# Two transformer-style blocks on one core: a new order for the opening, for three places in the middle and for the last two units

## The chip, the cores and the metric

The kernel runs on one core of a Trainium2 chip. The metric is device time in microseconds (us): the median of 3 runs of the kernel before is 921.19 us (920.6 to 923.35). All times in the rows are counted from the start of the span of one profiled execution.

Five engines work side by side, each in the order of its own program, and wait for each other by semaphores: PE (TensorE, the matmuls; PEld is its weight load), DVE (VectorE), ACT (ScalarE), POOL (GpSimd), and SP, which here only issues transfers. PE writes into eight banks of PSUM.

## The reference, cut to what matters

Everything is float32. The input is x of 256 positions by 1024 columns. The first block is

```
h = rms_norm(x, pre_mix);  proj = h @ w_in          # 3472 columns and a remainder of 16: gdn_a, gdn_b
o_att = attention(att_q, att_k, att_v, rel_bias)    # 8 heads, causal, one block of 256
qkv = silu(depthwise_conv4(gdn_qkv))                # 1536 columns
beta = sigmoid(gdn_b);  g = -exp(A_log) * softplus(gdn_a + dt_bias)      # "the gates", 8 heads
o_gdn = chunked gated delta rule over q, k, v, beta, cumsum(g)           # triangular solve, state
o_gdn = rms_norm(o_gdn per head) * norm_w * silu(z)                      # "the gated norm"
x = x + rms_norm([o_att, o_gdn] @ w_out, post_mix)
h = rms_norm(x, pre_mlp);  x = x + rms_norm(square(relu(h @ w_up)) @ w_down, post_mlp)
```

The second block is a gated convolution and a retention layer, mixed by w_o_2, and then

```
h2 = rmsnorm(x, g_ffn)
x = x + (silu(h2 @ w_ff_gate) * (h2 @ w_ff_up)) @ w_ff_down              # 11 tiles of 256 columns
return rmsnorm(x, g_final)
```

## The kernel before, in words

**Units.** The weights are cut into 144 units of 128 x 2048 values (the first, of kind Z, has 1024: the 128 columns that end with the gates' 16). SP loads unit after unit into three raw buffers. To keep the precision of float32, each unit is split: ACT casts it to a rounded leading part (`t_wh`, "hi", line 1100, or in two halves at line 1114), DVE subtracts (`t_wl`, "lo", line 1569, in halves at 1583). The activations are split in the same way into `t_hx` (hh and hl). Each product is three matmuls: leading by leading, leading by remainder both ways. ACT and DVE split units two ahead of the one that PE is at (`next_unit` in each engine's program); `t_wh` and `t_wl` have four buffers, so a split waits for PE only where it is four units ahead.

**Order.** There is no scheduler. Each engine's program is written out by hand, in one order, and a wait is set where an engine needs another's result. What an engine does late in its own order therefore holds up all that is written behind it.

**Banks.** PE asks for a bank with `take`. Without a number it gets the next of the banks 4 to 7 in rotation; with a number it gets that one. `opened` makes PE wait until the bank's last reader is done, and `drain` says who that reader is. Wide units first move the rotation to an even bank and take two.

**Opening (lines 580 to 636).** PE starts with 14 matmuls of constants (line 582), transposes the two scaled halves of x (`turn_x`, line 407, one half of the positions after the other), and makes a small matmul for the attention bias (line 590). Then come the unit Z, called "ab" here (line 430, 24 matmuls), and the six convolution units (48 matmuls each). ACT and DVE make hh and hl from the transposed x, eight products each (lines 1143 and 1595); each matmul step k waits for the k-th of DVE's. ab waits for its bank 4 too, whose last reader is DVE's second product. After convolution unit 0 PE transposes the gates (`t_dU`), and after unit 1 it sums them (lines 624 and 625). On DVE the gates' arithmetic stands behind the three taps of convolution unit 0 (1595), and on ACT behind that unit's copy and first tap (lines 1218, 1226), exps (1230 to 1234) and a logarithm (1236) with its table load.

**Middle.** The products kT with kq (line 701, eight banks' worth in four pairs, "KQ") are read by DVE, two operations per bank. The delta rule's inverse is made in levels with many 64 x 64 matmuls (726) between attention steps (660, 663, 686). `mend` (804) needs DVE's copy `t_cout` of line 1842 (`to_second_half`), which for c = 1 stands behind the gated norm of c = 0, and this norm contains a wait for a root on POOL (2172). `between` is the passage from one layer to the next, used twice ("mlp", "mix2"): ACT casts one unit in halves and one whole and then copies two banks (line 1178, to `t_up` or `t_vv`).

**End.** `a_pair` (line 515) makes the last two units of the feed-forward's down projection: 24 matmuls of tile t = 0 and then 24 of t = 1, in each of them 12 with the first unit and 12 with the second. The second unit needs `t_fl` of the last tile from DVE.

## Time and profile before

| | us |
|---|---|
| median of 3 runs | 921.19 (920.6 to 923.35) |
| profiled execution, its time | 920.38 |
| profiled execution, its span | 918.6 |
| PE busy | 898.2 (98%), 5456 matmuls |
| PEld busy | 764.6 (83%) |
| DVE busy | 603.1 (66%) |
| ACT busy | 461.0 (50%) |
| POOL busy | 91.0 (10%) |
| mean granted clock of TensorE | 0.996 |

The time contains 1.78 us outside the span (920.38 less 918.6). PE is idle for 20.4 us in all (918.6 less 898.2). In the rows below, a time in brackets is the idle time of the engine just before the instruction, with what released it; "x8" is a count of instructions merged into one row. A float32 matmul of constants or of another tile that is not rounded shows as two records.

### The profile page before, as it was taken

Reading aid. Unit: us, or ns where it says so; the run is one execution under the profiler, and the core shown is the slowest. Engines: PE = TensorE matmul, PEld = TensorE weight load, DVE = VectorE, ACT = ScalarE, POOL = GpSimd, SP = SyncE. Lnnn points to the kernel's source line nnn. Section 1 sums busy time; section 2 is a strip of 40 time slices with the busy share of each in tenths; the row PEclk is TensorE's granted clock in tenths of the full one; section 3 lists DMA queues with packets and bytes.
Section 4 is the critical chain, followed back from the end, with each engine's and each line's share of the span. In section 5 each row is a group of like instructions: output and inputs, shape, how many; then the busy total and the mean of one; then the engine's idle time right before and its main releaser. Section 6 shows DMA issues by size and latency. Waiting matters only on the chain.

```text
span 918.6 us, 12761 instructions
## 1 busy us (share of the span) xinstructions
PE 898.2 (98%) x5456; PEld 764.6 (83%) x5456; DVE 603.1 (66%) x704; ACT 461.0 (50%) x557; POOL 91.0 (10%) x92
## 2 busy tenths in 40 slices
PE   7999999999999999999999999999999999999996
PEld 7998888778888887888888878778788888888885
DVE  6689984676556667687767665556656656564655
ACT  6766365464445445654643354453455555444543
POOL 1124100100000000100034410110100000000000
PEclk9999999999999999999999999999999999999999
DMA  8635512335444455445474524544455346555531
GB/s 314 247 138 184 172 50 93 131 125 218 185 183 183 183 186 227 171 185 184 147 266 156 198 107 183 181 165 161 163 202 180 138 171 234 180 183 218 183 138 46
DMA packets 24217, 159.81 MB, mean 174 GB/s; under 512 B 3240, under 2 KB 3768, under 8 KB 5856
## 3 DMA queue, kind: packets, MB, share of 16 engines
q1 hardware_dynamic: 21600, 152.58, 45.6%
q0 software_dynamic: 2272, 6.24, 1.9%
q8 instruction: 43, 0.70, 0.3%
q10 hardware_dynamic: 288, 0.17, 0.1%
q14 instruction: 14, 0.11, 0.0%
HBM read 157.91 MB, written 2.63 MB: 175 GB/s over the span
## 4 chain that ended last, share of the span: by engine, by line
PE 76%; DVE 13%; ACT 6%; issue 2%; DMA 1%; POOL 1%; POOLq 0%; DVEq 0%; ACTq 0%
PE banks L490 32%; PE banks L458 20%; PE banks L461 10%; DVE t_wl L1569 5%; ACT t_wh L1100 2%; PE banks L515 2%; PE banks L430 2%; PE banks L726 2%; PE banks L980 1%; PE banks L407 1%; DVE t_cout L1595 1%; PE banks L570 1%; PE banks L930 1%; DVE t_hx L1595 1%; PE banks L1062 1%
## 5 line engine op out<-in xcount | busy, mean ns | idle before, releaser
L1569 DVE TENSOR_TENSOR t_wl<-t_raw,t_wh 128x2048 fp32r<-128x2048 f32 (+1 forms) x140 | 319.2, 2301 | 125.8 <-ACT t_wh L1100 124.6
L458 PE MATMUL banks<-t_hx,t_wh 128*128 128x512 f32 x992 | 312.2, 396 | 1.0 <-ACT t_vv L1178 0.5
L1100 ACT CAST t_wh<-t_raw 128x2048 fp32r<-128x2048 f32 (+1 forms) x140 | 262.6, 1900 | 12.0 <-DMA t_raw<-in_W 7.6
L461 PEld LDWEIGHTS banks<-t_hx,t_wl 128*128 128x128 f32 x992 | 186.3, 188 | 43.8
L461 PE MATMUL banks<-t_hx,t_wl 128*128 128x256 f32 x992 | 194.9, 278 | 0.0
L458 PEld LDWEIGHTS banks<-t_hx,t_wh 128*128 128x128 f32 x992 | 153.2, 189 | 4.0 <-DVE t_wl L1583 1.8
L490 PE MATMUL banks<-t_wh,t_hx 128*128 128x512 f32 x320 | 102.3, 396 | 0.0
L490 PEld LDWEIGHTS banks<-t_wh,t_hx 128*128 128x128 f32 x320 | 59.5, 188 | 12.7 <-issue 0.6
L430 PE MATMUL banks<-t_hx,t_wh 128*128 128x256 f32 x336 | 62.8, 289 | 1.5 <-DVE t_hx L1595 1.5
L490 PE MATMUL banks<-t_wl,t_hx 128*128 128x512 f32 x160 | 61.1, 390 | 0.0
L430 PEld LDWEIGHTS banks<-t_hx,t_wh 128*128 128x128 f32 x336 | 53.6, 196 | 2.6 <-DVE t_hx L1595 2.2
L2172 POOL TENSOR_TENSOR t_st<-t_st,t_half 128x1 f32<-128x1 f32 (+1 forms) x18 | 10.6, 589 | 435.0 <-DVE t_st L1595 433.2
L1419 ACT COPY t_hold<-banks 128x512 f32<-128x512 f32 x28 | 16.4, 584 | 68.6 <-PE banks L461 57.5
L430 PE MATMUL banks<-t_hx,t_wl 128*128 128x256 f32 x168 | 48.2, 287 | 0.0
L1378 ACT COPY t_tail<-banks 128x512 f32<-128x512 f32 x14 | 8.2, 586 | 55.6 <-PE banks L461 55.6
L490 PEld LDWEIGHTS banks<-t_wl,t_hx 128*128 128x128 f32 x160 | 30.1, 188 | 6.3 <-issue 0.2
L490 PE MATMUL banks<-t_wh,t_mh 128*128 128x512 f32 x112 | 34.6, 390 | 0.0
L490 PE MATMUL banks<-t_wl,t_mh 128*128 128x512 f32 x112 | 34.5, 389 | 0.0
L490 PE MATMUL banks<-t_wh,t_ml 128*128 128x512 f32 x112 | 34.5, 389 | 0.0
L430 PEld LDWEIGHTS banks<-t_hx,t_wl 128*128 128x128 f32 x168 | 32.9, 196 | 0.0
L1587 DVE TENSOR_TENSOR t_rl<-banks,t_tail 128x512 f32<-128x512 f32 x14 | 9.7, 690 | 28.4 <-ACT t_tail L1378 28.4
L2266 POOL TENSOR_SCALAR t_gt<-t_gt,t_small 128x256 f32<-128x256 f32 x16 | 14.6, 924 | 117.2 <-ACT t_gt L1477 105.3
(310 smaller groups left out, 1258.5 us busy)
## 6 DMA issues: line engine op xcount, KB each, us to landing
t_raw<-in_W SPq DMA_DIRECT2D x143, 1024.0 KB, 4.9
skew<-scr POOLq DMA_DIRECT2D x1, 1536.0 KB, 13.2
t_x<-in_x SPq DMA_DIRECT2D x2, 512.0 KB, 5.0
t_tab<-in_tab POOLq DMA_DIRECT2D x1, 640.0 KB, 6.1
out<-t_xt SPq DMA_DIRECT2D x2, 320.0 KB, 2.3
t_raw<-in_W SPq DMA_DIRECT2D x1, 512.0 KB, 6.8
t_T<-skew POOLq DMA_DIRECT2D x4, 128.0 KB, 2.4
t_xt<-skew POOLq DMA_DIRECT2D x4, 128.0 KB, 2.4
```

The source lines that it names most:

```text
L430: m = e.matmul(bank[b][:, c * S:c * S + S], W[w][:, h, k * 128 * nt + c * 128:k * 128 * nt + c * 128 + 128], H[a][:, k, :], start=first, s ...
L458: e.matmul(bank[b + c], M.wh[:, h, wk], M.hx[:, k, :, :].rearrange("p a s -> p (a s)"), start=k == 0, stop=False)
L461: m = e.matmul(bank[b + c][:, 0:S], M.wl[:, h, wk], M.hh[:, k, :], start=False, stop=k == 7)
L490: m = e.matmul(bank[outs[t][c]][:], act[a][:, ks[kk], t * 128:t * 128 + 128], W[w][:, h, kk * 512 * ncb + c * 512:kk * 512 * ncb + c * 512 ...
L515: m = e.matmul(bank[outs[t][c]][:], act[a][:, k, t * 128:t * 128 + 128], W[w][:, (i0 + u) % HR, kk * 1024 + c * 512:kk * 1024 + c * 512 + ...
L726: m = e.matmul(bank[b][p, i * 64:i * 64 + 64], left(p), right(p), start=True, stop=True)
L1100: e.copy(M.wh[:, h, 0:n], M.raw[:, r, 0:n]).then_inc(q.sem, q.tick(("hi", i)))
L1419: e.copy(halves(M.rest[:, s, :]), both(M.banks, at[tile], 1)).then_inc(q.sem, q.tick((tile, "rest")))
L1569: e.tensor_tensor(M.wl[:, h, 0:n], M.raw[:, r, 0:n], M.wh[:, h, 0:n].bitcast(F32), ALU.subtract).then_inc(q.sem, q.tick(("lo", i)))
L1595: return e.scalar_tensor_tensor(out=o, in0=a, scalar=s, in1=b, op0=op0, op1=op1).then_inc(q.sem, q.tick(*names))
L2172: return e.tensor_tensor(o, a, b, op).then_inc(q.sem, q.tick(*names))
L2266: e.tensor_scalar(M.gt[:, a, :], M.gt[:, a, :], gw[:, 4 * h + a:4 * h + a + 1], None, ALU.mult).then_inc(q.sem, q.tick(("gt", h, a)))
```

## The change

Eight edits, all of order and place; the products that reach the output are the same, and five matmuls of constants are added.

1. The 14 constant matmuls write bank 3 instead of 7. Four more stand between the transposes of the two halves of x, and one behind the bias matmul.
2. Unit Z (ab) takes bank 1 instead of the next in rotation. It is split in two halves of 512, by ACT and DVE. It and convolution unit 0 start on the leading halves (`hi`) and take the leading products of k = 0 to 3 first, then those with `t_wl`, then k = 4 to 7.
3. The gates are transposed in the middle of convolution unit 0, and their arithmetic on DVE and ACT stands ahead of that unit's taps and copy.
4. The bias tables lie in `t_PT` and `t_va` instead of `t_cout`, so ACT's taps wait neither for the bias row nor for its transfer; POOL clears the convolution's margin (`pad`) first.
5. KQ pairs 4 to 7 take the banks 0 to 3.
6. One cast of ACT moves from between two copies at level 1 of the inverse to between the two copies of `t_va`; in `between`, one cast moves to between the two copies of line 1178.
7. `to_second_half(1)` moves into the gated norm of c = 0, ahead of the wait for POOL's root.
8. In the last `a_pair`, six matmuls of t = 1 with the first unit stand ahead of the matmuls of t = 0 with the second (`ahead=6`).

Since ab and four KQ banks no longer come from the rotation, every bank taken from it up to the passage "mlp" is one place lower in the new kernel; from the wide units on both kernels have the same banks.

```diff
-            def b_unit(tile, arrived, by, name, kind="B", k_outer=False, mid=None, halved=False):
+            def b_unit(tile, arrived, by, name, kind="B", to=None, mid=None, halved=False):
...
-                q.wait_ge(DV, ("lo", i, 0) if halved else ("lo", i))
+                q.wait_ge(*((AC, ("hi", i, 0)) if halved else (DV, ("lo", i))))
...
+                if halved:
+                    order = steps(range(4), (0, 1)) + steps(range(4), (2,)) + steps(range(4, 8), range(3))
...
+                    if halved and n_ == 8 * nt:
+                        q.wait_ge(DV, ("lo", i, 0))
+                    elif halved and n_ == 12 * nt:
                         q.wait_ge(DV, ("lo", i))
...
+                order = [(t, n_) for t in range(2) for n_ in range(24)]
+                order = order[:12] + order[24:24 + ahead] + order[12:24] + order[24 + ahead:]
...
+            def constants(n):
+
+                q.wait_ge(PO, "half")
+                for i in range(n):
+                    e.matmul(bank[3][:, 0:128], M.half[:], M.half[:], start=True, stop=True)
...
+                    if t == 0:
+                        constants(4)
...
-            b_unit("ab", x_in, AC, "ab", "Z")
+            constants(1)
+            b_unit("ab", x_in, AC, "ab", "Z", to=1, halved=True)
...
-                b_unit(("conv", u), x_in, AC, ("cin", u), k_outer=u == 0, halved=u == 0,
-                       mid=queries_and_keys if u == 5 else None)
+                b_unit(("conv", u), x_in, AC, ("cin", u), halved=u == 0,
+                       mid=gates if u == 0 else queries_and_keys if u == 5 else None)
...
-                bs = [take(("KQ", g + w)) for w in range(2)]
+                bs = [take(("KQ", g + w), None if g < 4 else g + w - 4) for w in range(2)]
...
-                hi(unit[0] + 3)
-                unit[0] += 2
                 for t in range(2):
                     q.wait_ge(PE, ("first", g, t))
                     e.copy(dst[:, t, :], bank[at["first", g, t]][:]).then_inc(q.sem, q.tick(taken(t)))
+                    if t == 0:
+                        hi(unit[0] + 3)
+                        unit[0] += 2
...
                 e.copy(M.va[:, c, :], bank[at["va", c]][:]).then_inc(q.sem, q.tick(("va", c)))
+                if c == 0:
+                    next_unit()
...
                 if c:
                     lo_half(0)
+                else:
+                    to_second_half(1)
```

**PE's opening.** The names in the rows: `t_xt` is the scaled x, `t_hx` its transposed parts, `t_half` the constants; the row with 8x384 is the bias matmul, and the first row with `t_wh` opens ab. Before:

```order
L407 MATMUL banks<-t_ident,t_xt 128x128 [waits act_done]
L407 MATMUL banks<-t_ident,t_xt 128x128 x3
L407 MATMUL banks<-t_ident,t_xt 128x128 [waits dve_done]
L407 MATMUL banks<-t_ident,t_xt 128x128 x3
L407 MATMUL banks<-t_ident,t_xt 128x128 [waits act_done]
L407 MATMUL banks<-t_ident,t_xt 128x128 x3
L590 MATMUL banks<-t_cout 8x384 [waits in_rbT,in_onehot]
L430 MATMUL banks<-t_hx,t_wh 128x256 [waits dve_done]
L430 MATMUL banks<-t_hx,t_wh 128x256
L430 MATMUL banks<-t_hx,t_wl 128x256
```

In the new kernel the same place reads:

```order
L405 MATMUL banks<-t_ident,t_xt 128x128 x3
L543 MATMUL banks<-t_half 128x128 x4
L405 MATMUL banks<-t_ident,t_xt 128x128 [waits dve_done]
L405 MATMUL banks<-t_ident,t_xt 128x128 x3
L405 MATMUL banks<-t_ident,t_xt 128x128 [waits act_done]
L405 MATMUL banks<-t_ident,t_xt 128x128 x3
L601 MATMUL banks<-t_PT,t_va 8x384 [waits in_rbT,in_onehot]
L543 MATMUL banks<-t_half 128x128
L434 MATMUL banks<-t_hx,t_wh 128x256 [waits dve_done,act_done]
L434 MATMUL banks<-t_hx,t_wh 128x256
L434 MATMUL banks<-t_hx,t_wh 128x256 [waits dve_done]
L434 MATMUL banks<-t_hx,t_wh 128x256
```

Four and one constant matmuls have come in, and ab opens with pairs of leading matmuls, each pair with a wait of its own, where a matmul with `t_wl` stood third before.

**DVE around convolution unit 0.** `t_cout<-banks,t_cout` (new: `t_va<-banks,t_PT`) is the bias row, the rows of `t_wl` 128x2048 are the remainders of the units 2, 3 and 4, `t_gs` holds the gates, and `t_cout<-t_cin` are the taps. Before:

```order
L1587 TENSOR_TENSOR t_cout<-banks,t_cout 8x384 [waits in_neg,pe_done]
L1569 TENSOR_TENSOR t_wl<-t_raw,t_wh 128x2048 [waits act_done,raw_in2]
L1569 TENSOR_TENSOR t_wl<-t_raw,t_wh 128x2048 [waits act_done,raw_in0]
L1595 SCALAR_TENSOR_TENSOR t_cout<-t_cin,t_small,t_cout 128x256 [waits act_done] x2
L1595 SCALAR_TENSOR_TENSOR t_cout<-t_cin,t_small,t_cout 128x256 [waits dve_done] x4
L1587 TENSOR_TENSOR t_gs<-banks,t_small 128x16 [waits pe_done]
L1709 COPY t_gs<-banks 128x16
L1595 SCALAR_TENSOR_TENSOR t_gs<-t_gs 128x16 [waits dve_done]
L1591 TENSOR_SCALAR t_gs<-t_gs 128x16 [waits act_done]
L1715 RECIPROCAL t_gs<-t_gs 128x16 [waits dve_done]
L1595 SCALAR_TENSOR_TENSOR t_gs<-t_gs 128x16 [waits act_done]
L1595 SCALAR_TENSOR_TENSOR t_gs<-t_gs 128x16 [waits dve_done]
```

The same engine and place in the new kernel:

```order
L1600 TENSOR_TENSOR t_va<-banks,t_PT 8x384 [waits in_neg,pe_done]
L1582 TENSOR_TENSOR t_wl<-t_raw,t_wh 128x2048 [waits act_done,raw_in2]
L1600 TENSOR_TENSOR t_gs<-banks,t_small 128x16 [waits pe_done]
L1706 COPY t_gs<-banks 128x16
L1608 SCALAR_TENSOR_TENSOR t_gs<-t_gs 128x16 [waits dve_done]
L1582 TENSOR_TENSOR t_wl<-t_raw,t_wh 128x2048 [waits act_done,raw_in0]
L1604 TENSOR_SCALAR t_gs<-t_gs 128x16 [waits act_done]
L1715 RECIPROCAL t_gs<-t_gs 128x16 [waits dve_done]
L1608 SCALAR_TENSOR_TENSOR t_gs<-t_gs 128x16 [waits act_done]
L1608 SCALAR_TENSOR_TENSOR t_gs<-t_gs 128x16 [waits dve_done]
L1608 SCALAR_TENSOR_TENSOR t_cout<-t_cin,t_small,t_cout 128x256 [waits act_done] x2
L1608 SCALAR_TENSOR_TENSOR t_cout<-t_cin,t_small,t_cout 128x256 [waits dve_done] x4
```

The gates stand around the remainder of unit 3 and ahead of the six taps.

**DVE at the gated norm.** `t_gs<-t_kb` is the sum of squares, `t_cin<-t_cin,t_gs` the first product after POOL's root, and `t_cout<-banks 64x512` the copy that `mend(1)` needs. Before:

```order
L1866 TENSOR_REDUCE t_gs<-t_kb 128x8 [waits act_done]
L1591 TENSOR_SCALAR t_gs<-t_gs 128x8 [waits dve_done]
L1587 TENSOR_TENSOR t_cin<-t_cin,t_gs 128x512 [waits pool_done]
L1587 TENSOR_TENSOR t_cin<-t_cin 128x512 [waits dve_done]
L1842 COPY t_cout<-banks 64x512 [waits pe_done]
L1569 TENSOR_TENSOR t_wl<-t_raw,t_wh 128x2048 [waits act_done,raw_in1]
```

and in the new kernel:

```order
L1880 TENSOR_REDUCE t_gs<-t_kb 128x8 [waits act_done]
L1604 TENSOR_SCALAR t_gs<-t_gs 128x8 [waits dve_done]
L1856 COPY t_cout<-banks 64x512 [waits pe_done]
L1600 TENSOR_TENSOR t_cin<-t_cin,t_gs 128x512 [waits pool_done]
L1600 TENSOR_TENSOR t_cin<-t_cin 128x512 [waits dve_done]
L1582 TENSOR_TENSOR t_wl<-t_raw,t_wh 128x2048 [waits act_done,raw_in1]
```

The copy has moved up by two places, to the front of the wait for POOL.

## Rows read from the trace of the kernel before

**Rows 1.** The page, part 1: busy us, share of the span, instructions.
```profile
PE 898.2 (98%) x5456; PEld 764.6 (83%) x5456; DVE 603.1 (66%) x704; ACT 461.0 (50%) x557; POOL 91.0 (10%) x92
```

**Rows 2.** Waits of PE: engine, tile, line, releaser: us in total, times, longest.
```profile
PE banks L430 <- DVE t_hx L1595: 1.5, 1, 1.5
PE banks L804 <- DVE t_cout L1842: 1.4, 1, 1.4
...
PE banks L701 <- DVE t_dU L1587: 0.9, 2, 0.7
PE banks L515 <- DVE t_fl L1587: 0.9, 1, 0.9
...
PE banks L624 <- DVE t_gs L1595: 0.8, 1, 0.8
...
PE banks L458 <- ACT t_vv L1178: 0.5, 1, 0.5
...
PE banks L660 <- ACT t_xt L1311: 0.4, 1, 0.4
```

**Rows 3.** Matmuls of line 430 in three stretches: us, busy (count), PEclk, DMA.
```profile
12.84:23.07 10.23, 10.20 (x72) 10.18 (x72) 0.83 0.86 324
14.24:17.62 3.38, 3.38 (x18) 3.38 (x17) 0.51 0.75 305
23.20:29.20 6.00, 6.00 (x49) 5.79 (x48) 1.00 0.85 320
```

**Rows 4.** Timeline of the opening: start us, us, instruction [idle before <-releaser].
```profile
9.58 1.03 ACT L1100 CAST t_wh<-t_raw 128x1024 fp32r<-128x1024 f32 x1
...
10.71 1.23 DVE L1569 TENSOR_TENSOR t_wl<-t_raw,t_wh 128x1024 fp32r<-128x1024 f32 x1 [1.27 <-ACT t_wh L1100]
11.86 3.22 DVE L1595 SCALAR_TENSOR_TENSOR t_hx<-banks,t_small,t_hx 128x256 fp32r<-128x256 f32 x8
...
12.87 0.47 PE L430 MATMUL banks<-t_hx,t_wh 128*128 128x256 f32 x2 [1.55 <-DVE t_hx L1595]
...
17.22 0.37 ACT L1192 COPY t_dU<-banks 128x256 f32<-128x256 f32 x1
...
17.73 4.47 DVE L1569 TENSOR_TENSOR t_wl<-t_raw,t_wh 128x2048 fp32r<-128x2048 f32 x2
```

**Rows 5.** Timeline around the gates.
```profile
24.70 2.47 DVE L1595 SCALAR_TENSOR_TENSOR t_cout<-t_cin,t_small,t_cout 128x256 f32<-128x256 f32 x6 [2.50 <-ACT t_cout L1226]
...
27.94 1.28 ACT L1236 ACT_TABLE_LOAD   x1
...
30.01 0.36 PE L624 MATMUL banks<-t_gs,t_tab 128*128 128x16 f32 x2 [0.81 <-DVE t_gs L1595]
```

**Rows 6.** Two stretches: us, busy of PE, PEld, DVE, ACT, POOL, PEclk, DMA.
```profile
20.00:40.00 20.00, 19.19 (x160) 19.01 (x160) 12.21 (x24) 11.70 (x20) 3.45 (x6) 1.00 0.78 289
40.00:60.00 20.00, 20.00 (x168) 19.82 (x167) 18.99 (x39) 16.08 (x24) 0.00 (x0) 1.00 0.45 160
```

**Rows 7.** Timeline of PE where convolution unit 5's output is needed.
```profile
65.28 0.88 PE L407 MATMUL banks<-t_ident,t_cout 128*128 128x128 f32 x6 [0.56 <-ACT t_cout L1198]
```

**Rows 8.** Timeline where the inverse begins.
```profile
116.17 1.22 DVE L1587 TENSOR_TENSOR t_xt<-t_kb,t_tab 128x1024 f32<-128x1024 f32 x1
...
118.27 2.08 PE L726 MATMUL banks<-t_tab,t_xt 64*64 64x64 f32 x64
```

**Rows 9.** Timeline of ACT at level 1 of the inverse.
```profile
130.18 1.90 ACT L1100 CAST t_wh<-t_raw 128x2048 fp32r<-128x2048 f32 x1
```

**Rows 10.** Timeline of the gated norm of c = 0.
```profile
159.78 1.67 POOL L2172 TENSOR_TENSOR t_gs<-t_gs,t_half 128x8 f32<-128x8 f32 x1 [8.44 <-DVE t_gs L1591]
...
162.94 0.69 DVE L1842 COPY t_cout<-banks 64x512 f32<-64x512 f32 x1
```

**Rows 11.** Timeline of ACT at the end of the passage "mlp".
```profile
196.72 1.07 ACT L1178 COPY t_up<-banks 128x512 f32<-128x512 f32 x2
```

**Rows 12.** Timeline of DVE in the last stretch.
```profile
911.21 0.69 DVE L1587 TENSOR_TENSOR t_x<-t_x,banks 128x512 f32<-128x512 f32 x1 [1.19 <-PE banks L515]
```

188 lines of the change are left out of this document (90 added, 98 removed).

## The prediction, made before the changed kernel had run

> **What bounds the kernel now.** I read the page's first part for the busiest engine, then the waits of PE, then the timeline around each wait, and the windows for the clock. PE is busy for 898.2 of 918.6 us [rows 1]; the other engines matter only where PE waits for them. The reader is to see in the waits of PE that its 20.4 idle us are many small ones, of which seven kinds stand where this change has an edit [rows 2]. The windows show a loss that no wait shows: the granted clock is 0.51 from 14.24 to 17.62 us, the level of 1.2 GHz, and 1.00 afterwards, 2.4 GHz [rows 3]. So the time is a chain of PE's work, its short waits and one slow stretch, and I count what each edit takes out of this chain, and then whether another engine can follow.
>
> **Term 1, the opening (edits 1, 2 and 4): 2.0 us.** ab starts at 12.87 [rows 4]. DVE's eight products start at 11.86, when the remainder of unit Z is done, and last 3.22, 0.40 each [rows 4]. ab waits for two of them, since its bank 4 is read by the second. In the new kernel ACT casts 512 columns first. A cast of 1024 takes 1.03 and the DVE remainder 1.23 [rows 4]; half of each, with some 0.1 of fixed cost, is 0.6 and 0.65. The cast starts at 9.58, so the remainders run from 10.2 to 11.5 instead of 10.71 to 11.9, and the products start 0.35 earlier. Bank 1 is free, so ab waits for one product: 0.4 less. ab can then begin at 12.1, but each step waits for its product, and the last one is done at 11.5 + 3.22 = 14.7; three matmuls of 0.12 (6.00 us for 49, [rows 3]) and the way through the array end ab at 15.2. Convolution unit 0 follows with 48 x 0.12 = 5.76, and the gates' two transposes of some 0.25 together now stand inside it: unit 1 begins at 21.2 instead of 23.2 (72 matmuls in 10.23 us [rows 3], the transposes and their wait included behind them). Of these 2.0 us, 1.5 are the clock: 72 matmuls at 0.12 would take 8.7, not 10.2. The other 0.5 is the earlier start. Cover: unit 0's leading casts and first remainders are made by then (ACT has cast units 1 and 2 by 17.22, [rows 4]). The gates' transposes need ab's copy, which ACT makes at 17.22, behind these casts [rows 4]; PE comes to them at 15.2 + 24 x 0.12 = 18.1, so 0.9 us of cover is left, or 0.7 if the split cast costs ACT 0.2. Unit 1 needs the remainder of unit 2, which DVE starts at 17.73 and has after half of 4.47, at 20.0 [rows 4], before 21.2. The four constant matmuls stand in a pause of 1.2 us between the transposes and cost nothing unless the clock is low there; bounds 0 to 0.4. Edit 4 takes waits from ACT only, which is idle again before PE needs it; POOL's clearing comes before loads that PE does not wait for now, so I count nothing. Bounds of the term: 0.5 to 2.3.
>
> That the clock stays up is the open point. It fell at 14.24 after a stretch in which PE had only transposes, one bias matmul and pauses (the one before ab is 1.55, [rows 4]). Now five more matmuls lie in it, and ab starts 0.8 sooner. The Trainium skill, page "TensorE: Matmul & The Clock Gate", Part 4: PE-mode transpose, says that transposes do not count as work for the clock; the trace agrees in so far as the clock fell behind them. The same page, Part 1: The HAM clock gate, says that the points at which the clock is decided do not start with the kernel, so that the same kernel shows a different number of slow matmuls from run to run. This speaks against the edit: by this rule some executions would keep the slow stretch and pay the 1.5 us, and some of the kernel before would not have had it; no row here shows more than one execution.
>
> **Term 2, the gates (edit 3): 0.8 us.** PE waits 0.81 for the gates before line 624 [rows 5]. They stand on DVE behind the taps (24.70, 2.47 us) and on ACT lead to a table load of 1.28 [rows 5]. In the new order the gate transposes are done at 18.4, and DVE takes them after the remainder of unit 2 at 20.0. With ACT's exps, the table load and the rest (0.6 + 1.3 + 0.4, with DVE's next remainder of 2.3 beside them) the gates are ready near 23.3; PE asks at 21.2 + 5.8 = 27.0. The wait goes, with 3.7 us to spare. Queued behind the gates now are unit 0's copy and taps: ACT copies at 22.2 what PE has at 21.2, one us late; nobody needs these before the third transposes near 52. ACT and DVE split unit 4 some 4 us sooner than before, since its cast stood behind the logarithm. Bounds 0.5 to 0.8.
>
> **Does the chain follow?** These 2.8 us have to pass 40 to 65, where DVE is busy for 18.99 of 20 us; in the 20 before, it has 7.8 idle [rows 6]. Those idle times came from casts that stood behind the gates on ACT, so DVE enters the dense stretch earlier, by 3 or more. PE's wait at 65.28 for ACT's silu, 0.56 [rows 7], stays, shifted. I let the whole 2.8 pass.
>
> **Term 3, KQ's banks (edit 5): 0.8 us.** PE waits 0.9 in two pieces for DVE's products (line 701 [rows 2]). With banks 0 to 3 all four pairs run in a row. But DVE is then the chain: its table for the inverse runs from 116.17 for 1.22 to 117.4, and PE begins there at 118.27 [rows 8]. Only 0.88 can be gained, and this lies so near to 0.9 that I take 0.8. Bounds 0 to 0.9.
>
> **Term 4, the cast at level 1 (edit 6, first half): 0.4 us.** ACT's cast of 1.90 at 130.18 [rows 9] stands ahead of the copy for which PE waits 0.4 (line 660 [rows 2]). Moved between the copies of `t_va`, it lies in a pause of 2.1 us between them. Bounds 0 to 0.5.
>
> **Term 5, mend (edit 7): 1.4 us.** PE waits 1.4 for the copy at 162.94 [rows 2, 10]. POOL's root runs from 159.78 to 161.45 [rows 10] while DVE stands; the copy of 0.69 fits in, its input from PE being there at some 160.7. It ends at 161.5, when PE is still at its matmuls. What comes late next is nothing on this chain: the norm's products start at 161.5 instead of 161.49. Bounds 0.7 to 1.4.
>
> **Term 6, the two passages (edits 5 and 6): 1.0 us.** PE waits 0.5 each time for line 1178, for `t_vv` in this row and for as long for `t_up` [rows 2]. The wide unit's bank is the one of copy 0, and the copies stand behind a cast, at 196.72 [rows 11]. In "mlp" the shift of the banks alone takes the wait away (copy 0 now has bank 7, the wide unit 4 and 5); in "mix2" both have bank 4 still, and the cast's place does it. The second copy moves from 197.3 to some 197.5, while PE needs it at 198.4. Bounds 0.5 to 1.0.
>
> **Term 7, the end (edit 8): 0.8 us.** PE waits 0.9 for `t_fl` [rows 2]. Six matmuls of 0.225, 1.35 us, lie in it now. Tile 0 is done 0.45 later, tile 1 0.9 earlier. DVE's sum for tile 1 at 911.21 waits 1.19 for PE [rows 12], so it can follow by 0.8 once tile 0's work on it has moved. Bounds 0.4 to 0.9.
>
> **Sum.** 2.0 + 0.8 + 0.8 + 0.4 + 1.4 + 1.0 + 0.8 = 7.2 us. The profiled execution took 920.38 us, of which 918.6 are the span; 920.38 - 7.2 = 913.2. The median of the runs, 921.19, lies 0.8 above it, so in terms of medians I forecast 914.0. With all upper bounds the sum is 7.8, and 913.4.
>
> **Rivals.**
> - *The clock falls all the same.* Term 1 shrinks to 0.5, the sum to 5.7: 915.5 us. For it: the pauses before the transposes stay. Against: ab's start is denser with leading pairs only.
> - *DVE absorbs the opening.* If DVE's dense stretch from 40 to 65 does not begin earlier, PE arrives 2.8 sooner at 65.28 and waits as much longer, and KQ's 0.8 goes the same way into the wait for the inverse. Left are 3.6: 917.6. For it: 18.99 of 20 us [rows 6]. Against: the idle 7.8 before. With the low clock in addition nothing more is lost here, but if the last three terms also come at their lower bounds (1.6 instead of 3.2) 919.2 is left, no measurable change.
> - *The clock falls later and stays down.* This ends slower. PE would run ab at the pace of the products, 0.24 of work in each 0.40 at first, and the decision could fall in the dense convolution units. A slow matmul takes 3.38 / 16 = 0.21 (18 in the row less two that lie over its ends), 0.09 more than a fast one [rows 3]. It decides from 80 slow matmuls on, where 7.2 us are lost; at 120, two and a half units, 10.8 are lost, and with them the 2.8 us that make a slower verdict are reached: 921.19 - 7.2 + 10.8 = 924.8. Against: the clock was back from 17.62 on, with PE dense as it will be here [rows 3].
> - *Half of the change does not do what it says:* edit 6 in "mlp" is worth nothing, as worked out in term 6; that changes no sum.
>
> **How the numbers follow.** About 0.3%, 2.8 us, is what a measurement of this kernel tells from no change: faster is below 918.4, slower above 924.0. Forecast with the clock up: 0.47. Clock falls all the same: 0.20. Absorbed: 0.18. Absorbed and the last terms small, or gains lost to waits that I don't see: 0.11. Clock down for long: 0.04. The first three are faster, 0.85; same 0.11; slower 0.04. The range goes from 912.2 (the forecast's upper bound of the sum, 913.4, less the 1.2 by which a median can lie lower) to 918.6, just above the absorbed case. It leaves out some 0.17.
>
> **What would show it.** In the profile of the changed kernel: no stretch of 0.51 in PEclk and about 72 matmuls in 8.7 us from 12.1 on (term 1; a fall elsewhere in the first 30 us shows the rival). No wait of PE before the sums of the gates, and ACT's logarithm before its copy of unit 0 (term 2). The wait at 65.28 near 62.4 and not above 0.7 (if it is 3, the gain was absorbed). No wait at KQ and one of up to 0.4 before the inverse (term 3). No waits of PE for line 1178's and 1842's copies; the last output transfer 0.8 sooner behind the last wide unit. The forecast is wrong if the span is above 914 or if a new wait of PE over 0.5 us stands anywhere that these rows do not name.

## The result, and the profile after

The changed kernel takes 912.32 us (median of 4 runs, 912.14 to 912.44). The kernel before took 921.01 in the same comparison (920.6 to 923.35). The ratio is 0.9903, with a 95% interval of [0.989, 0.9915]. The forecast of 914.0 named the direction and the places; its sum of 7.2 us was too small. The medians differ by 8.7 us, the profiled spans by 8.1 (918.6 and 910.5). Even the sum of all upper bounds, 7.8, is less than that; 912.32 lies inside the range, whose lower end is 912.2, only by the 1.2 us that the range left for a lower median.

The first part of the page of the changed kernel, to be set against [rows 1]:

```profile
PE 898.0 (99%) x5466; PEld 765.9 (84%) x5466; DVE 602.7 (66%) x705; ACT 461.4 (51%) x558; POOL 90.9 (10%) x92
```

PE's busy time is the same: the slow stretch is gone, and the five constants came (ten records, two for each). What shrank is the idle time, from 20.4 to 12.5 us. Not all of that is time gained: 2.2 us of it are at the opening's transposes (`t_xt`, 3.2 before and 1.0 after), where PE now works on constants: the first 14 last 5.83 us instead of 4.84 in this execution, and the four new ones 1.06. The waits of PE in the changed kernel, against [rows 2]:

```profile
PE banks L405 <- DVE t_xt L1604: 1.0, 3, 0.6
...
PE banks L739 <- issue: 0.8, 1, 0.8
PE banks L739 <- DVE t_xt L1600: 0.5, 1, 0.5
PE banks L434 <- ACT t_hx L1157: 0.4, 1, 0.4
PE banks L405 <- ACT t_cout L1213: 0.4, 1, 0.4
```

Of the seven kinds of wait that [rows 2] shows, six are gone, and the one before ab is 0.4 instead of 1.5. One that was foretold is new: 0.5 before the inverse (line 739), where DVE's table is last now. The idle time of 0.8 at line 739, for which the profile names no releaser, was 0.5 before and is 0.5 when the changed kernel is profiled again. The opening's matmuls (line 434, which was 430) in one stretch, against the first of [rows 3]; the columns are us, busy PE (count), a second time for the weight loads, PEclk, DMA share, GB/s:

```profile
11.90:21.20 9.30, 9.26 (x72) 8.91 (x73) 1.00 0.89 344
```

The clock is 1.00 throughout this stretch. The timeline at places that answer to [rows 4, 5, 7, 8, 10]; the columns are start, us, instruction, and in brackets the idle time before it:

```profile
10.04 1.29 DVE L1596 TENSOR_TENSOR t_wl<-t_raw,t_wh 128x512 fp32r<-128x512 f32 x2 [0.85 <-ACT t_wh L1128]
11.31 3.23 DVE L1608 SCALAR_TENSOR_TENSOR t_hx<-banks,t_small,t_hx 128x256 fp32r<-128x256 f32 x8
...
11.94 0.69 PE L434 MATMUL banks<-t_hx,t_wh 128*128 128x256 f32 x3 [0.44 <-ACT t_hx L1157]
...
20.24 1.28 ACT L1240 ACT_TABLE_LOAD   x1
...
22.25 0.91 ACT L1248 ACTIVATE t_cout<-t_cin,t_small 128x256 f32<-128x256 f32 x2
...
62.03 0.88 PE L405 MATMUL banks<-t_ident,t_cout 128*128 128x128 f32 x6 [0.37 <-ACT t_cout L1213]
...
83.00 3.72 PE L714 MATMUL banks<-t_cout 64*128 64x256 f32 x32
...
114.11 2.08 PE L739 MATMUL banks<-t_tab,t_xt 64*64 64x64 f32 x64 [0.49 <-DVE t_xt L1600]
...
156.54 0.69 DVE L1856 COPY t_cout<-banks 64x512 f32<-64x512 f32 x1 [1.08 <-PE banks L807]
157.27 0.69 DVE L1600 TENSOR_TENSOR t_cin<-t_cin,t_gs 128x512 f32<-128x512 f32 x1
```

The reader is to see: ab starts 0.93 earlier. The table load for the logarithm stands ahead of unit 0's taps. The wait for ACT's silu, at 65.28 before, comes at 62.03 and is 0.37 long, so the gain has passed DVE's dense stretch. All of KQ runs in one row of 32. DVE's copy for mend lies in the pause of the norm, whose product follows without a gap.

How far PE is ahead of the kernel before, from start times in the two profiles: 0.93 at the first ab matmul, 1.94 at unit 1, 2.99 at the sums, 3.26 at KQ, 4.16 at the inverse, 4.58 at S6 and 4.23 at the second unit after it, 5.67 at the second mend, 6.29 at the first wide unit of the MLP, 6.99 in mix2, 7.07 at the last pair, 8.1 at the end.

### The profile page after: what moved, and what is told of

It reads as the page before. It is cut to its first block, busy times and chain, and to the rows that moved or that the text cites. A ratio compares the mean times of both kernels' runs of the same rounds, so it can differ in the third digit from the quotient of the medians.

```text
span 910.5 us, 12778 instructions
## 1 busy us (share of the span) xinstructions
PE 898.0 (99%) x5466; PEld 765.9 (84%) x5466; DVE 602.7 (66%) x705; ACT 461.4 (51%) x558; POOL 90.9 (10%) x92
## 4 chain that ended last, share of the span: by engine, by line
PE 80%; DVE 12%; ACT 4%; issue 2%; DMA 0%; POOL 0%; POOLq 0%; DVEq 0%; ACTq 0%
PE banks L494 31%; PE banks L462 20%; PE banks L465 10%; DVE t_wl L1582 4%; PE banks L434 4%; PE banks L585 3%; PE banks L522 2%; PE banks L739 2%; PE banks L993 2%; PE banks L405 1%; ACT t_wh L1114 1%; DVE t_hold L1600 1%; DVE t_xt L1600 1%; PE banks L943 1%; PE banks L1075 1%
## 5 line engine op out<-in xcount | busy, mean ns | idle before, releaser
L1582 DVE TENSOR_TENSOR t_wl<-t_raw,t_wh 128x2048 fp32r<-128x2048 f32 x139 | 318.0, 2309 | 123.2 <-ACT t_wh L1114 121.9
L1114 ACT CAST t_wh<-t_raw 128x2048 fp32r<-128x2048 f32 x139 | 261.5, 1906 | 12.8 <-DMA t_raw<-in_W 8.1
L434 PE MATMUL banks<-t_hx,t_wh 128*128 128x256 f32 x336 | 60.6, 285 | 0.4 <-ACT t_hx L1157 0.4
```

What stands on the lines that cost most here:

```text
L434: m = e.matmul(bank[b][:, c * S:c * S + S], W[w][:, h, k * 128 * nt + c * 128:k * 128 * nt + c * 128 + 128], H[a][:, k, :], start=first, s ...
L1114: e.copy(M.wh[:, h, 0:n], M.raw[:, r, 0:n]).then_inc(q.sem, q.tick(("hi", i)))
L1582: e.tensor_tensor(M.wl[:, h, 0:n], M.raw[:, r, 0:n], M.wh[:, h, 0:n].bitcast(F32), ALU.subtract).then_inc(q.sem, q.tick(("lo", i)))
```

## The experiments

A time in brackets is the range of a kernel's executions. The changed kernel's 912.22 in the first of these comparisons is what "one edit undone" is compared with; the other comparisons ran on other chips. The kernel before had medians from 920.7 to 920.98 in all five of them, so differences under 0.3 us are not read, and those of 0.4 or 0.5 with caution.

**The changed kernel again.**

> The changed kernel itself, as the yardstick for the other runs of this call. Both theories: 912.3 +- 0.3 us, with a granted clock near 0.999 in every run, where the kernel before shows 0.996 or less in some.

912.22 us (911.9 to 912.82), ratio 0.9887 [0.9865, 0.9908]; span 910.1. The kernel before, beside it, ran from 919.89 to 925.62. Over five such comparisons it has 76 times: 42 below 921.1, 22 from there to 923, 12 above, median 920.8. So the kernel before scatters upward by up to 5 us and the changed one by 1. The forecast had taken the distance of 0.8 between profile and median as fixed; it is this scatter, and half of it came from a median of three, 921.19, where 76 give 920.8.

**The opening's constants.**

```diff
-                    if t == 0:
-                        constants(4)
...
-            constants(1)
```

> The changed kernel without its five added constant matmuls (the fourteen at the start stay). Theory A, the constants keep the clock up: PEclk falls once between 10 and 20 us for about 3.4 us, 16 slow matmuls, and the time is 1.0 to 1.6 us above the changed kernel (913.3 to 913.9). Rival B, ab's earlier and denser start is enough: no fall, time within 0.2 us of the changed kernel. Rival C, the fall is a matter of each execution: some runs 1.5 above, some equal.

Without them 912.79 (911.84 to 914.35), 0.6 more. Its profile shows the fall in the opening:

```profile
10.00:12.00 2.00, 1.20 (x7) 0.90 1.00 422
12.00:14.00 2.00, 1.94 (x9) 0.50 1.00 416
14.00:16.00 2.00, 2.00 (x15) 0.75 1.03 436
```

The mean granted clock of its six executions goes with their times, 0.999 for the two fastest and 0.994 for the slowest: by this, the fall happens in some executions and not in others. The fall of this profile costs less than the 1.5 us that were counted for the clock: PE starts unit 1 at 22.29, 1.03 later than in the changed kernel (21.26); probably because ab goes at the pace of DVE's products for a part of it. At KQ it is still 1.03 behind (84.03), at the second mend 0.5 (158.28 against 157.77 in the second profile of the changed kernel), because the idle time of 0.5 in the inverse that has no releaser is not there.

> The kernel before with the five constant matmuls and nothing else. Theory A: the slow stretch goes and the time falls by 1.0 to 1.6 us below the kernel before. Rival B: no change, the slow stretch stays since ab still starts late. Rival C: the spread of the kernel before (920.6 to 923.4) stays.

The kernel before with the constants alone became slower: 923.64 (920.76 to 926.46), ratio 1.0021 [1.0003, 1.0039]. Theory A expected the opposite. In its profile the opening had clock 1.00, and PE then stood longer before the sums, after which the clock fell. The wait, the timeline row and the windows from its profile:

```profile
PE banks L631 <- DVE t_gs L1602: 1.6, 1, 1.6
```

```profile
29.64 0.37 PE L631 MATMUL banks<-t_gs,t_tab 128*128 128x16 f32 x2 [1.61 <-DVE t_gs L1602]
```

```profile
28.00:30.00 2.00, 0.39 (x5) 1.00 0.51 210
30.00:32.00 2.00, 2.00 (x17) 0.85 0.50 205
32.00:34.00 2.00, 2.00 (x11) 0.50 0.55 216
34.00:36.00 2.00, 2.00 (x16) 0.79 0.87 263
```

Behind the wait of 1.61 us the clock falls, for some 3.4 us in all (an estimate from the shares 0.85, 0.50 and 0.79 in these rows). In this execution the fall has moved from the opening to behind the wait. PE is at the sums 0.37 earlier than in the kernel before, and the fall then costs 1.3: the transposes of `t_cout` that wait for ACT's silu start 36.59 after the sums instead of 35.27. The other 2 us by which the median lies above this execution's 921.7 are not in this profile.

**The gates' place.** The gates' block goes back behind the first unit on PE and behind its taps on ACT and DVE.

```diff
-                       mid=gates if u == 0 else queries_and_keys if u == 5 else None)
-                if u == 1:
+                       mid=queries_and_keys if u == 5 else None)
+                if u == 0:
+                    gates()
+                elif u == 1:
```

> The changed kernel with the gates put back: transposed behind convolution unit 0, their arithmetic on DVE and ACT behind that unit's taps. Theory A: PE waits again before the sums, 0.8 us, or up to 2.9 if DVE and ACT have not moved with PE's earlier arrival: time 0.8 to 1.6 us above the changed kernel. Rival D, the gates' place also sets when the casts run ahead and with it the rest of the chain to 65 us: more than 2 us above.

913.08 (912.68 to 913.32), 0.9 more; the sums wait 0.5.

**Terms 3 to 7, one edit undone at a time.**

```diff
-                bs = [take(("KQ", g + w), None if g < 4 else g + w - 4) for w in range(2)]
+                bs = [take(("KQ", g + w)) for w in range(2)]
```

> The changed kernel with one edit undone: the banks of KQ(4) to KQ(7) come from the rotation again. Prediction's step: TensorE waits again 0.7 us before KQ(6) for DVE's product t_dU and 0.2 us after it, and nothing before the inverse gives it back: 0.8 us more than the changed kernel's 912.2, 913.0. Rival (DVE's inverse table bounds the start of the inverse anyway): the wait returns, but the wait of 0.5 us for t_xt ahead of the first inverse matmul goes, so 0.2 to 0.4 us more, 912.5. Rival for the bank shift: with the old banks the passage of the MLP (two 0.5 us waits of line 458 in the kernel before, for ScalarE's copies) comes back as well, which adds up to 0.5 us: 913.5.

912.94 (912.73 to 913.31), 0.7 more. The waits of 0.7 and 0.2 for `t_dU` are back, the 0.5 before the inverse is gone. The MLP passage has no wait, so these banks don't cover it.

```diff
-                else:
-                    to_second_half(1)
...
             gated_norm(0)
+            to_second_half(1)
```

> The changed kernel with one edit undone: VectorE does the casts of the second half before the pause of the gated norm, not in it. Prediction's step: the wait of TensorE for t_cout (1.4 us in the kernel before) returns, and stays in the sum to the end: 1.4 us more, 913.6. Rival (later waits absorb it): the wait of line 458 and the passages after it wait for ScalarE, which isn't moved, so of the 1.4 us part is given back before the first wide unit: 0.5 to 0.9 us more, 912.9.

913.76 (912.99 to 915.17), 1.5 more. Its profile is one of the two long executions, span 913.3, and shows the wait of 1.35 us and a fall of the clock behind it, which costs 1.6 between the mend and the MLP's first wide unit (34.73 us instead of 33.11).

```profile
158.00:160.00 2.00, 0.74 (x12) 1.00 0.24 98
160.00:162.00 2.00, 2.00 (x13) 0.84 0.00 0
162.00:164.00 2.00, 2.00 (x8) 0.50 0.75 188
164.00:166.00 2.00, 2.00 (x13) 0.81 0.80 336
```

```diff
                 hi_halves()
+                hi(unit[0] + 3)
+                unit[0] += 2
...
-                    if t == 0:
-                        hi(unit[0] + 3)
-                        unit[0] += 2
```

> The changed kernel with one edit undone: in both passages ScalarE casts the high half of unit + 3 ahead of both copies of the values again. Prediction's step: 0.5 us returns in mix2's passage (line 458's wait for t_vv), and in the MLP's passage nothing, since the shift of banks alone took that wait: 0.5 us more, 912.7. Rival: the wait of the MLP's passage was taken by this edit and not by the banks: 0.5 us at either place, 1.0 us more, 913.2.

912.72 (912.57 to 912.87), 0.5 more. Only mix2's wait is back, for `t_vv`.

```diff
-                   ahead=6)
+                   ahead=0)
```

> The changed kernel with one edit undone: the last pair of units runs in its old order, with none of the second token tile's matmuls ahead. Prediction's step: the wait of 0.9 us ahead of line 515's third group, for DVE's t_fl, returns, and the last drain starts that much later: 0.8 to 0.9 us more, 913.1. Rival (the end of the kernel hangs on the last copy and its DMA, not on TensorE): under 0.3 us more, 912.4. The changed kernel gained 1.0 us between the start of this pair and the end, against 0.8 forecast; if all of it is this order, 1.0 returns.

913.24 (913.1 to 913.5), 1.0 more, with the wait of 0.9 for `t_fl`.

**Filling the waits.** These two are to separate the idle time from the fall behind it. Constants stand where PE would idle.

```diff
+                    for i in range(6):
+                        e.matmul(bank[b][:, 0:128], M.half[:], M.half[:], start=True, stop=True)
                     q.wait_dma(LD["tab"])
                     q.wait_ge(DV, "graw")
```

> The kernel before with the five constants in its opening and six more of them (128x128 each) ahead of the cumulative sums, where the kernel with five waited 1.6 us for the gates and the granted clock then fell to 0.5 for 4 us (its windows of 30 to 36 us). The six write the sums' own bank before the sums do, and take no wait away. Theory D (TensorE's idling brings the clock down): 6 x 0.21 us fill 1.3 of the 1.6 us, the clock stays at 1.00 in 30 to 36 us, and the profiled span is 1.5 to 2.0 us below the 919.9 of the kernel with five: 918.2; the time's median falls from 923.6 to 921 or 922. Rival E (the clock falls there for another reason, such as the load as a whole, and filling only adds work): the fall stays or moves on, span 919.9 to 920.2, median 923.6 or more.

921.09 (919.8 to 925.33), 2.5 less than the kernel with five constants; span 918.4. Two of these twelve executions are above 923; of the twelve without the six constants, eight were. Its windows in the opening and at the same place:

```profile
12.00:14.00 2.00, 1.41 (x7) 0.70 0.97 405
14.00:16.00 2.00, 2.00 (x12) 0.50 1.07 439
...
28.00:30.00 2.00, 2.00 (x20) 1.00 0.55 221
30.00:32.00 2.00, 1.74 (x15) 1.00 0.54 221
32.00:34.00 2.00, 2.00 (x19) 1.00 0.52 209
```

With six useless matmuls in it, this wait (1.5 us of constants and 0.26 idle) has no fall behind it. But two things weaken that reading. The opening has a fall here in spite of its five constants; of the four profiles with these five in the old order it is the only one, while all five profiles without them have one in the opening, and none of the eleven with the new order and the constants. And a wait with nothing in it can go without a fall as well: the second profile of the kernel before (below) waits 1.50 us for the gates and keeps its clock:

```profile
30.00:32.00 2.00, 0.72 (x6) 1.00 0.52 212
32.00:34.00 2.00, 2.00 (x19) 1.00 0.51 207
```

So filling is supported by the times (8 of 12 against 2 of 12) more than by the windows. The next puts five of them ahead of the second mend, in the kernel with the mend edit undone:

```diff
+                if c:
+                    f = 4 + turn[0] % 4
+                    opened(f)
+                    for i in range(5):
+                        e.matmul(bank[f][:, 0:128], M.half[:], M.half[:], start=True, stop=True)
                 q.wait_ge(DV, ("zt", c))
```

> The changed kernel with VectorE's cast of the second half back in its old place (the wait of 1.35 us before the second mend is there again), and five constants (128x128, into a free bank) ahead of that mend. Without the five, its profiled execution had the clock at 0.5 in 162 to 165 us and a span of 913.3, two of its five executions were near 915 and three between 913.0 and 913.8. Theory D (idling brings the clock down, in some executions): the five fill 1.1 us of the wait, the clock stays at 1.00, all executions lie between 912.9 and 913.8, profiled span 911.3. Rival E: the fall goes on at times whatever is done with the wait: some executions near 915, and the median 913.8 or more.

913.57 (912.86 to 913.7), none of six near 915. Clock 1.00 from 156 to 168 us, span 911.5:

```profile
157.57 1.27 PE L818 MATMUL banks<-t_half 128*128 128x128 f32 x10
159.09 1.14 PE L822 MATMUL banks<-t_cout,t_xt 64*64 64x64 f32 x16 [0.24 <-DVE t_cout L1861]
```

This does not show that the filling did it. The same wait of 1.35 us, with nothing in it, stands in nine profiles (before and its repeat, and seven variants), and the clock fell behind it in one of them, the one above. The next kernel has it too, and its six executions lie within 0.4 us.

**Do the terms add up?** Edits 5 to 8 undone together, that is the four diffs above (KQ, mend, casts, last pair) and the cast at level 1.

> The changed kernel with edits 5 to 8 undone together (KQ banks, cast at level 1, cast of the second half, casts between the copies, order of the last pair), so that only the new opening and the gates ahead are left. If the terms add up as measured one by one (0.7, 0.4 as forecast, 1.5, 0.5 and 1.0): 912.2 + 4.1 = 916.3. If the terms overlap, so that one wait takes up another: 915.5. If the upper group of the kernel before (its executions near 925) comes from the opening, no execution here lies over 918.5; if it comes from behind the opening, some lie near 920.

916.37 (916.14 to 916.55), as in the sum, which however holds 0.4 for the cast; the run below gives 0.0 for it, so the parts as measured make 3.7 of the 4.15. Its MLP passage has no wait for `t_up`, though its casts and KQ's banks are the old ones.

```diff
+                        if (l, g) == (1, 0):
+                            next_unit()
...
-                if c == 0:
-                    next_unit()
```

> The changed kernel with one edit undone: ScalarE's cast of a unit's high half stands again in level 1 of the inverse, ahead of a copy. Prediction's step: TensorE waits 0.4 us more there, and the time is 0.4 us more: 912.6. Rival (in the changed kernel the inverse waits for DVE instead, so the copy isn't late): no change, 912.2. Rival (the cast runs into the copies of S6 as well): 1.0 us more, 913.2.

912.27 (912.11 to 912.51), no change, although PE waits 0.4 for ACT again and stands 0.7 later at the next units. At 358 us PE waits for DVE's `t_xt` for 0.23 instead of 0.58, which gives 0.35 of it back; by 450 us 0.3 is left against the first profile of the changed kernel and 0.6 against the second.

**What makes the upper executions?** First the opening's new order, banks, tables and padding without constants and without the gates' new place.

> The kernel before with the new order and bank of the ab unit and its casts in halves (with the bias tables' and the padding's new places) alone: no added constants, gates behind the first convolution's unit, the five later edits undone. The opening with constants and gates ahead gave 916.4, and taking the constants and the gates' place from the whole changed kernel cost 0.6 and 0.9 us. If the three parts add up: 916.4 + 1.5 = 917.9, and no execution over 919.5. Theory D with the waits as they stand then (the sums' wait for the gates of 0.5 us and more behind a slow opening, the second mend's of 1.35 us): a fall of the clock in some executions, which makes them 2 us longer, and a median of 918 to 920. If the upper group is something of the old order of the ab unit, none lies over 921; if it is of the constants' or the gates' place, some lie at 921 to 924.

918.38 (917.88 to 919.03), ratio 0.9967 [0.9954, 0.998]: no upper executions among six, 0.5 above the sum of the parts. The slow stretch is still in its opening (0.83 in 10 to 20 us), and the mean clock is 0.996 in all six, so the 2.6 us below the kernel before are not the missing fall. Then the kernel before with all eleven constants and the mend edit:

> The kernel before with five constants in the opening, six ahead of the cumulative sums, and VectorE's cast of the second half in the pause of the gated norm: every place at which a fall of the clock was seen is filled or has lost its wait. The same without the moved cast had a median of 921.1 and executions up to 925.3. Theory D: 1.4 us of wait and the falls go: median 918.6, none over 921. Rival (the upper group is no matter of the clock): the lower group goes to 918.5, and some still lie 3 to 5 us above it, with a mean granted clock as high as the others'.

919.2 (918.18 to 921.75). Theory D wanted none above 921, and its profile has the sums waiting 2.2 us at full clock, so something else makes that wait long. The next two are one execution each:

> The kernel before, unchanged, profiled once more. Of its 43 executions beside the earlier runs some two in ten lay above 923. If this profile is one of them, it shows in which stretch the 3 to 5 us are lost: theory D expects windows of 2 us with a clock of 0.5 behind the sums (30 to 36 us) or behind the second mend (165 to 170 us), the rival a wait or a slower stretch at full clock.

921.57 us, span 919.8, with a longer slow stretch in the opening (0.66 in 10 to 20 us, where the first profile had 0.83).

> The kernel before with the five constants, profiled once more; half of its twelve executions lay above 923.5. Theory D expects a fall behind the sums' wait, as in its first profile (span 919.9), and in an upper execution a second one behind the mend's wait of 1.4 us (span 922); the rival a wait or a slower stretch at full clock.

925.51 us, span 923.7: one of the upper group. PE waits 4.1 us for the gates. The timeline shows where they come from:

```profile
17.82 0.53 POOL L2209 DMA_DIRECT2D scr<-t_cout  x1 [8.53 <-DVE t_cout L1594]
24.87 1.11 POOL L2211 DMA_DIRECT2D skew<-scr  x1 [6.52 <-DMA scr<-t_cout]
25.97 0.15 POOL L2212 MEMSET t_cin<- 128x36 f32 x1
...
26.21 0.91 ACT L1233 ACTIVATE t_cout<-t_cin,t_small 128x256 f32<-128x256 f32 x2 [3.57 <-POOL t_cin L2212]
...
32.05 0.58 PE L631 MATMUL banks<-t_gs,t_tab 128*128 128x16 f32 x2 [4.07 <-DVE t_gs L1602]
```

POOL sends the bias row (12 KB) to memory and waits for it to land, and only then clears the padding of `t_cin`; ACT's first tap waits for that, and the gates stand behind the taps. In the first profile of this same kernel, span 919.9, the transfer landed sooner, and the wait was 1.61:

```profile
22.46 1.11 POOL L2211 DMA_DIRECT2D skew<-scr  x1 [4.04 <-DMA scr<-t_cout]
...
23.79 0.91 ACT L1233 ACTIVATE t_cout<-t_cin,t_small 128x256 f32<-128x256 f32 x2 [1.10 <-POOL t_cin L2212]
```

The kernel before has the same chain in its first profile, short enough to be read over:

```profile
22.82 1.11 POOL L2204 DMA_DIRECT2D skew<-scr  x1 [4.20 <-DMA scr<-t_cout]
23.92 0.16 POOL L2205 MEMSET t_cin<- 128x36 f32 x1
...
24.16 0.91 ACT L1226 ACTIVATE t_cout<-t_cin,t_small 128x256 f32<-128x256 f32 x2 [0.31 <-POOL t_cin L2205]
```

How firmly the sums hang on the tap can be read from all nine profiles in which the gates stand behind the taps: the sums start 5.84 to 5.86 us after the first tap in each (29.64 and 23.79 above, 32.05 and 26.21, 30.01 and 24.16 in the kernel before), whether the opening had its slow stretch or not. The kernel with the new order alone, where edit 4 has cut the tap loose from the transfer, is the counter-test: there the transfer landed latest of all, and the tap and the sums do not feel it.

```profile
22.79 0.91 ACT L1237 ACTIVATE t_cout<-t_cin,t_small 128x256 f32<-128x256 f32 x2
...
24.95 1.11 POOL L2217 DMA_DIRECT2D skew<-scr  x1 [6.83 <-DMA scr<-t_va]
...
28.65 0.37 PE L636 MATMUL banks<-t_gs,t_tab 128*128 128x16 f32 x2 [0.55 <-DVE t_gs L1606]
```

In the upper execution the clock then falls behind the 4 us of nothing:

```profile
30.00:32.00 2.00, 0.00 (x0) 1.00 0.52 212
32.00:34.00 2.00, 1.95 (x9) 0.51 0.51 207
34.00:36.00 2.00, 2.00 (x11) 0.50 0.13 51
36.00:38.00 2.00, 2.00 (x12) 0.50 0.57 139
```

Edit 4 alone, made to the kernel before and then undone in the changed one:

```diff
-        M.oh = cout1[0:32, 0:384]
...
+            M.oh, M.ng = M.PT[0:32, 0, :], M.PT[0:8, 1, :]
...
-                q.wait_dma(LD["scr"])
-                q.wait_ge(DV, "row")
...
+            e.memset(M.cin[:, :, 0:3], 0.0).then_inc(q.sem, q.tick("pad"))
             e.dma_start(M.oh, A["onehot"]).then_inc(LD["onehot"], 16)
```

> The kernel before with one thing changed: the padding of t_cin stands first on GpSimd, ahead of all DMAs, the bias tables lie in t_PT and t_va and no longer in t_cout, and ScalarE's first tap no longer waits for the bias row's DMA. Theory F (that DMA's landing, 4.3 to 7.1 us after its issue in the profiles so far, sets the first tap and so the gates and the sums): the wait before the first tap goes (0.31 us in the profile of before, 1.0 and 3.6 in other executions), the sums' wait is 0.5 us in every execution, none lies over 922.5 (a fall of the clock behind the second mend alone may add 2 to 920.3), and the median is 920.3. Rival D (the upper executions are falls of the clock): some still lie from 923 to 926, the median stays at 920.8 or more.

920.03 (919.16 to 922.41, 12 executions), ratio 0.9991 [0.9979, 1.0002]; the tap at 23.28 waits for nothing, the sums 0.5. None is above 922.5; the kernel before had 2 of 17 above 924 beside it. By themselves twelve executions are few for that, and the median's gain of 0.7 is not certain: the interval holds 1.

> The changed kernel with that one edit undone: the padding behind the bias row's DMA, the tables in t_cout, the first tap waiting for the landing. The gates are computed ahead of the taps there, so a late landing can't hold the sums up by the gates, only by VectorE's taps: theory F with the gates apart: the first tap starts up to 2.5 us late, the taps of unit 0 on VectorE (2.47 us) and what is behind them move by that, TensorE waits for them at the transposes near 27 to 60 us only if VectorE has less than that to spare: 912.2 to 913.5, with a spread of over 1 us. Rival (the gates' place covers it wholly): 912.2, spread as in the changed kernel (0.9 us).

911.83 (911.54 to 912.33), ratio 0.9892 [0.9874, 0.991]: nothing is lost (0.4 less than 912.22, on another chip). In its profile the tap starts at 23.29, 1.04 later than in the changed kernel, and the sums at 26.90 wait for nothing. So with the gates ahead of the taps a tap that is 1.04 late holds up nothing that PE needs soon; the transfer landed early here (4.2 us after its issue), and a late one in this kernel was not seen. As far as these runs go, edit 4 is worth something only where the gates stand behind the taps.

## Why the prediction was right and where it failed

What each term gave, in us: at its place in the changed kernel's profile, and as the median that undoing it cost.

| term | forecast | in the profile | undone |
|---|---|---|---|
| 1 opening | 2.0 | 1.94 | constants 0.6, tables and padding 0.0; the rest not undone |
| 2 gates | 0.8 | 1.05 | 0.9 |
| 3 KQ's banks | 0.8 | 0.90 | 0.7 |
| 4 cast at level 1 | 0.4 | 0.42 | 0.0 |
| 5 mend | 1.4 | 1.44 | 1.5 |
| 6 passages | 1.0 | 0.62 and 0.70 | 0.5 (mix2) |
| 7 end | 0.8 | 1.0 | 1.0 |

Terms 3 and 5 stand as worked out; term 7 gave 1.0 against an upper bound of 0.9. Borne out too is "the chain follows": PE was 2.99 ahead at the sums and 3.26 at KQ, so DVE's dense stretch took nothing. The wait that takes the place of KQ's (0.5 before the inverse) came where it was foretold. Term 4 was right at its place and wrong at the end. I had let it pass undiminished; undone, it costs nothing, and 0.35 of it is given back in PE's wait at 358 us. Another 0.35 of the 4.58 gained at S6 is lost before mend, in the idle time without a releaser; the second profile of the changed kernel does not lose it, so that is the execution and not the term.

The total of term 1 came out by compensation, which is luck. Of its 2.0 us, 1.5 were counted for the clock and 0.5 for the earlier start; from the kernel without the added constants, whose profile has the fall, the clock is 1.03 at unit 1 (22.29 and 21.26) and the earlier start 0.91 (23.20 and 22.29).

Where the span's gain of 8.1 exceeds the sum of 7.2, the milestones place it: 0.25 at the sums, 0.27 between them and KQ, 0.32 at the two passages, 0.2 at the end, less the 0.35 lost before mend, and small ones. A removed wait gave somewhat more than its row: the MLP's 0.49 gave 0.62, the sums' 0.81 gave 1.05. So terms 2, 6 and 7, each priced by the row of its wait, were set too low.

Two steps failed.

**"Edit 4 takes waits from ACT only [...] so I count nothing."** ACT was said to be idle again before PE needs it. But ACT's first tap waits for the bias row's DMA by way of POOL, and the gates, for which PE waits, stand behind the tap. In two executions of one kernel (that with five constants) POOL stood 4.04 and 6.52 us for that DMA, PE waited 1.61 and 4.07 us for the gates, and the spans were 919.9 and 923.7; with edit 4 in, a landing as late left the wait at 0.55. The price of edits 1 to 4 was thus not that of the one profile I had. The opening with the gates gave 4.4 us between medians (920.74 and 916.37) where 2.8 were forecast; edits 5 to 8 gave 4.15 where 3.9 were (4.4 less 0.5 for the MLP passage, which belongs to the opening, below). So the opening has 1.1 of the miss in the sum, even with that 0.5 added to its forecast. Roughly, across two comparisons: 2.6 come with the order, banks, tables and padding (920.98 and 918.38), and 2.0 more with constants and gates (918.38 and 916.37). The 2.6 hold no missing fall, as said above; in that profile PE is 1.36 ahead at the sums and 0.65 more at the MLP. Moving the tables and the padding alone gave 0.7 by its median, and that is not certain; how the rest divides into the missing late landing and the earlier start is not separated further.

**"The median of the runs lies 0.8 above it", added to the sum.** The distance was treated as a constant of the kernel. It was the kernel's own scatter (and the small number of three executions). A late landing is shown as one source of it; a fall of the clock behind a pause is seen in profiles of variants, and for the kernel before itself it is inferred. The change takes the tap's wait and the pause before mend away, and the changed kernel's median (912.32) lies on its profiled execution's time (912.35). This step alone is 0.8 of the 1.7 us by which 914.0 was off; the rest is 8.1 of span against 7.2.

A smaller one: term 6 named the right reason for "mlp", a shift of banks, but the wrong edit. Taking KQ(4) to KQ(7) out of a rotation of four shifts nothing. The shift is ab's (`to=1`): the MLP's wait is gone with edits 5 to 8 undone. The half of term 6 belongs to the opening.

Of the rivals, "the clock falls all the same" is what happens in some executions without the constants, and in the profile the fall lay between 10 and 16 us. It cost 0.6 in the median and 2.1 in the slowest of the six executions, where the rival's price was 1.5. In the whole changed kernel no execution looks like it: the ten that ran lie within 1 us, and the mean granted clock of the six in the second comparison was 0.998 or 0.999. The prediction had cited the Trainium skill, "TensorE: Matmul & The Clock Gate", Part 1: The HAM clock gate, for slow matmuls that differ in number from run to run; the runs here agree for the kernel before (clock 0.83 and 0.66 in 10 to 20 us of its two profiles) and not for the changed one. "The clock falls later" was ruled out by pointing at dense work behind the opening; in the kernel with constants alone it did fall later, in a wait that had not been looked at as a cause. It stayed low for some 3.4 us only. "DVE absorbs the opening" is refuted by the milestones.

## What to carry to other kernels

A wait of TensorE costs its length, a little more (0.49 in the row gave 0.62 here), and in some executions a fall of the clock behind it: 1.3 and 1.6 us behind waits of 1.61 and 1.35 here, though eight other profiles with the wait of 1.35 had none. A few matmuls on constants in such a wait may buy that back (8 of 12 long executions became 2 of 12 before the sums); before the mend this was not shown. Before an edit is counted at nothing because its engine "is idle anyway", follow who waits for that engine through the semaphores, and ask of each DMA in that chain how long it takes in other executions than the profiled one. If a kernel's times scatter, profile it again until an upper execution is caught: one such profile here named a cause that the comparisons of medians had not. And look for an interval that stays the same in every profile, like the 5.85 us from the first tap to the sums: it tells which chain sets a start.

## What the runs showed of the hardware that was not expected

- Behind waits of 1.61 and 1.35 us the granted clock went to 0.5 for some 3.4 us (around 32 to 34 and 162 to 164 us above), in the middle of a kernel that otherwise keeps PE at 98 or 99%; behind a wait of 1.50, and behind 1.35 in eight other profiles, it stayed at 1.00. After 4 us of nothing it was at 0.5 from 32 to 38 us at least.
- Removing a fall of the clock can make the kernel slower: with five constants in the opening, 923.64 against 920.7 us. In the profile PE came to the sums only 0.37 earlier, since their start is set by the first tap, and a fall behind the wait cost 1.3. The rest of the 2.9 was not followed; late landings of the bias row are one part that was seen.
- A DMA of 12 KB from SBUF to memory, issued from POOL while the units were being loaded, took from 4.2 to 7.1 us from issue to landing in the twenty profiles of these kernels: 4.2 to 4.4 in twelve, 6.0 or more in six. Two executions of the same kernel had 4.3 and 6.8, two of the kernel before 4.4 and 6.0.
